# Decay sums of the second block's mixer as 16-row products in two row groups, two head pairs together

## The reference

```
dt = softplus(dt + dt_bias);  a = dt * a_neg                 # per token and head
a_cs = cumsum(a) within a chunk
cb   = einsum('bclgn,bcsgn->bcgls', cc, bc)
m    = cb * exp(where(l >= s, a_cs[l] - a_cs[s], -inf))      # decay between tokens s and l
y    = einsum(m, xs * dt)  (+ what comes over the chunk's border, + d_skip * xs)
y    = rmsnorm(y * silu(z)) ;  out = concat(attn, y) @ w_out
```

## Time and profile before

| what | value |
|---|---|
| median of three runs | 1451.77 us (1451.28 to 1452.57) |
| the profiled execution's own time | 1452.29 us |
| its span | 1450.5 us |
| TensorE busy | 1439.6 us, 99% |
| VectorE busy | 917.8 us, 63% |
| ScalarE busy | 803.5 us, 55% |
| granted TensorE clock, mean | 0.999 |

### The profile page before, as it was taken

One profiled execution on the slowest core, in us unless ns is written; L12 is line 12 of the kernel. 1 busy time (PEld: TensorE's weight loads), 2 busy tenths in 40 slices (PEclk: granted clock), 3 DMA queues, 4 the chain that ended last, 5 costly groups with the idle time before them and its releaser, 6 DMA issues.

```text
span 1450.5 us, 20440 instructions
## 1 busy us (share of the span) xinstructions
PE 1439.6 (99%) x8050; PEld 1228.2 (85%) x8050; DVE 917.8 (63%) x1269; ACT 803.5 (55%) x1301; POOL 78.5 (5%) x86
## 2 busy tenths in 40 slices
PE   9999999999999999999999999999999999999998
PEld 8888888888888888888889988888888998888886
DVE  5697765565557877555555778655555678655554
ACT  6775554444467654544445786544445687554443
POOL 0113100000002230000000000000000000000001
PEclk9999999999999999999999999999999999999999
DMA  8644456656375436565664434576564434465661
GB/s 280 214 155 129 144 166 202 201 189 191 91 236 175 145 118 188 175 204 189 189 189 131 133 116 131 174 215 208 183 193 125 155 118 146 154 206 182 188 189 54
DMA packets 178703, 245.49 MB, mean 169 GB/s; under 512 B 18976, under 2 KB 130224, under 8 KB 178608
## 3 DMA queue, kind: packets, MB, share of 16 engines
q1 hardware_dynamic: 178416, 244.11, 53.7%
q10 hardware_dynamic: 192, 0.08, 0.0%
HBM read 243.10 MB, written 1.05 MB: 168 GB/s over the span
## 4 chain that ended last, share of the span: by engine, by line
PE 93%; DVE 3%; ACT 2%; issue 1%; DVEq 0%; ACTq 0%
PE acc L556 18%; PE acc L559 17%; PE acc L562 17%; PE misc L556 10%; PE misc L559 10%; PE misc L562 10%; PE misc L655 3%; DVE w_lo L1404 2%; PE misc L694 1%; PE misc L912 1%; PE misc L718 1%; ACT w_hi L1001 1%; PE misc L852 1%; PE misc L663 1%; ACT arena L1068 1%
## 5 line engine op out<-in xcount | busy, mean ns | idle before, releaser
L1404 DVE TENSOR_TENSOR w_lo<-w_raw,w_hi 128x1024 fp32r<-128x1024 f32 (+3 forms) x472 | 557.2, 1195 | 295.5 <-ACT w_hi L1001 293.2
L1001 ACT ACTIVATE w_hi<-w_raw 128x1024 fp32r<-128x1024 f32 (+3 forms) x472 | 479.2, 1030 | 276.3 <-PE misc L562 164.1
L556 PE MATMUL acc<-w_hi,h_hi 128*128 128x512 f32 (+3 forms) x832 | 208.7, 373 | 1.0 <-ACT w_hi L1001 1.0
L559 PE MATMUL acc<-w_lo,h_hi 128*128 128x512 f32 (+3 forms) x832 | 201.0, 364 | 0.2 <-DVE w_lo L1404 0.2
L562 PE MATMUL acc<-w_hi,h_lo 128*128 128x512 f32 (+3 forms) x832 | 201.0, 364 | 0.0
L556 PE MATMUL misc<-w_hi,h_hi 128*128 128x512 f32 x640 | 175.6, 396 | 0.0
L559 PE MATMUL misc<-w_lo,h_hi 128*128 128x512 f32 x640 | 171.6, 390 | 0.0
L562 PE MATMUL misc<-w_hi,h_lo 128*128 128x512 f32 x640 | 171.5, 390 | 0.0
L559 PEld LDWEIGHTS acc<-w_lo,h_hi 128*128 128x128 f32 x832 | 147.9, 188 | 22.6 <-DVE w_lo L1404 0.7
L562 PEld LDWEIGHTS acc<-w_hi,h_lo 128*128 128x128 f32 x832 | 148.0, 188 | 21.6
L556 PEld LDWEIGHTS acc<-w_hi,h_hi 128*128 128x128 f32 x832 | 142.5, 189 | 21.7 <-ACT w_hi L1001 1.1
(11 more groups left out here) (221 smaller groups left out, 1217.0 us busy)
## 6 DMA issues: line engine op xcount, KB each, us to landing
w_raw<-in_w_in SPq DMA_DIRECT2D x92, 512.0 KB, 4.1
w_raw<-in_w_gate SPq DMA_DIRECT2D x176, 256.0 KB, 2.9
w_raw<-in_w_up SPq DMA_DIRECT2D x176, 256.0 KB, 3.1
w_raw<-in_w_down SPq DMA_DIRECT2D x88, 512.0 KB, 3.5
w_raw<-in_w_out SPq DMA_DIRECT2D x40, 512.0 KB, 3.9
w_raw<-in_w_in SPq DMA_DIRECT2D x32, 388.0 KB, 3.5
w_raw<-in_w_in SPq DMA_DIRECT2D x16, 336.0 KB, 4.2
w_raw<-in_w_proj_a SPq DMA_DIRECT2D x8, 512.0 KB, 4.1
```

What stands on the lines that cost most here:

```text
L556: pe.matmul(dst, st[0][:, k, t * P:(t + 1) * P], rhs, start=first, stop=False)
L559: pe.matmul(dst, st[0][:, k, t * P:(t + 1) * P], rhs, start=False, stop=False)
L1001: act.activation(w_hi[:, g % RING, 0:w], w_raw[:, g % RING, 0:w], ACT.Copy)\
L1404: dve.tensor_tensor(w_lo[:, g % RING, 0:w], w_raw[:, g % RING, 0:w], w_hi[:, g % RING, 0:w].bitcast(F32), ALU.subtract)\
```

## The change

The running sums are also computed the other way round in cs: four products with 16 columns of `dt_a` as weights and `tri` moving give 16 rows (heads) by 256 tokens, once at rows 0 to 15 and once at rows 64 to 79 of cs's bank. VectorE copies both to a new tile `csT`. A head's row is then spread to all 128 rows by a product of 16 rows: one column of the identity, broadcast to 128 weight columns, with `csT`, 256 columns moving. Two pairs are done in one call, alternating between row groups 0 and 64 and the pairs' two banks; the calls for odd pairs are empty. In `order` cr comes in twos, and z1 stands between y0 and cr2. `reader` makes the bank of cs wait for `csT`. VectorE does `exponents` two by two, and the split counts of both engines are changed to fit.

```diff
--- before.py
+++ after.py
@@ -171,8 +171,8 @@
     order = """
         nT0 nT1 qkv0 nT2 nT3 qkv0 qkv1 qkv1 cvT0 cvT1 qkv2 qkv2 xd0 xd0 qkT0 qkT1 qkT2 qkT3 qkT4 xd0 S0 S1 xd0
         xd1 xd1 PT0 PT1 S2 S3 xT0 xd1 O0 O1 xd1 xd2 PT2 PT3 S4 S5 xd2 O2 O3 xT1 xd2 xT2 xd2 PT4 PT5 xd3 O4 O5
-        xd3 attT0 attT1 xT3 xd3 xd3 z0 xT4 xT5 z0 cs z0 z0 xsT0 xsT2 xsT1 xsT3 cr0 z1 cb0 cb1 cr1
-        z1 y0 cr2 z1 y1 cr3 z1 y2 cr4 wo0 y3 cr5 wo0 y4 cr6 wo1 y5 cr7 ssT0 ssT1 wo1 y6 y7 wo0 wo0 wo1
+        xd3 attT0 attT1 xT3 xd3 xd3 z0 xT4 xT5 z0 cs z0 z0 xsT0 xsT2 xsT1 xsT3 cr0 cr1 z1 cb0 cb1
+        z1 y0 z1 cr2 cr3 y1 z1 y2 wo0 cr4 cr5 y3 wo0 y4 wo1 cr6 cr7 y5 ssT0 ssT1 wo1 y6 y7 wo0 wo0 wo1
         ssT2 ssT3 wo1 wo0 wo0 wo1 mT0 mT1 wo1 mT2 mT3"""
     slots = {n: whole(n) for n in ch}
     plan = [slots[n].pop(0) if n in ch else ("misc", n) for n in order.split()]
@@ -253,6 +253,8 @@
 def reader(block, name):
     if block == 0 and name.startswith("oH"):
         return "dve", name
+    if name == "cs":
+        return "dve", "csT"
     if name in [f"S{g}" for g in range(6)]:
         return "dve", f"Sread{name[1:]}"
     return ("act", f"xs{name[3:]}") if name.startswith("xsT") else ("act" if name.startswith(ACT_READS) else "dve", name)
@@ -328,6 +330,7 @@
         rows = sb("rows", [P, P])
         conv = sb("conv", [P, 60])
         arena = sb("arena", [P, 26112])
+        csT = sb("csT", [P, T])
         acc = [ctx.enter_context(nc.psum_tensor(f"acc{i}", [P, 512], F32)) for i in range(4)]
         misc = [ctx.enter_context(nc.psum_tensor(f"misc{i}", [P, 512], F32)) for i in range(4)]
         ident = const[:, C_ID:C_ID + P]
@@ -843,14 +846,27 @@
                     b = bank_of(layer, name)
                     pe.matmul(b[:, 0:16], tri, dt_a[:, 0:16], start=True, stop=True)
                     pe.matmul(b[:, 16:32], tri, dt_a[:, 16:32], start=True, stop=True)
-                    pe.matmul(b[:, 32:48], bc(tri[:, P - 1:P], [P, P]), dt_a[:, 0:16], start=True, stop=True)\
-                        .then_inc(*PE.mark(name))
+                    pe.matmul(b[:, 32:48], bc(tri[:, P - 1:P], [P, P]), dt_a[:, 0:16], start=True, stop=True)
+                    for t in range(NT):
+                        for r0 in (0, 64):
+                            mm = pe.matmul(b[r0:r0 + SH, 64 + t * P:64 + (t + 1) * P], dt_a[:, 16 * t:16 * t + 16],
+                                           tri, start=True, stop=True)
+                    mm.then_inc(*PE.mark(name))
                 elif kind == "cr":
-                    b = bank_of(layer, name)
-                    for n, (hd, t) in enumerate((hd, t) for hd in (2 * i, 2 * i + 1) for t in range(NT)):
-                        a = dt_a[:, 16 * t + hd:16 * t + hd + 1]
-                        mm = pe.matmul(b[:, n * P:(n + 1) * P], bc(a, [P, P]), tri, start=True, stop=True)
-                    mm.then_inc(*PE.mark(name))
+                    if i % 2:
+                        return
+                    if i == 0:
+                        pe.wait_ge(*DV_.at(layer, "csT"))
+                    banks = [bank_of(layer, f"cr{i + k}") for k in range(2)]
+                    last = []
+                    for u in range(2):
+                        for k in range(2):
+                            r0, hd = 64 * k, 2 * (i + k) + u
+                            last.append(pe.matmul(banks[k][:, u * T:(u + 1) * T],
+                                                  bc(ident[r0:r0 + SH, r0 + hd:r0 + hd + 1], [SH, P]),
+                                                  csT[r0:r0 + SH, :], start=True, stop=True))
+                    last[-2].then_inc(*PE.mark(name))
+                    last[-1].then_inc(*PE.mark(f"cr{i + 1}"))
                 elif kind == "y":
                     pe.wait_ge(*DV_.at(layer, f"M{i}"))
                     if i in (0, 4):
@@ -1282,7 +1298,7 @@
 
                     j = PAIRS.index(hp)
                     if hp:
-                        split_until(layer, ORD[1].before["misc", f"cr{hp}"] + (2 if hp == 1 else LOOK))
+                        split_until(layer, ORD[1].before["misc", f"cr{hp}"] + (0, 3, LOOK - 1, LOOK - 1, LOOK, LOOK, LOOK, LOOK)[hp])
                     b = misc[ORD[1].turn[f"cr{hp}"] % 4]
                     act.wait_ge(*DV_.at(layer, f"cr{hp}"))
                     E = Ex[j % 3]
@@ -1857,7 +1873,9 @@
                 convolve(4)
                 dve.wait_ge(*PE.at(layer, "cs"))
                 b = misc[ORD[1].turn["cs"] % 4]
-                dve.tensor_copy(cs, b[:, 0:48]).then_inc(*DV_.mark("cs"))
+                dve.tensor_copy(cs, b[:, 0:48]).then_inc(*DV_.mark())
+                for r0 in (0, 64):
+                    dve.tensor_copy(csT[r0:r0 + SH, :], b[r0:r0 + SH, 64:64 + T]).then_inc(*DV_.mark("csT"))
                 dve.wait_ge(*AC.at(layer, "log_dt"))
                 dve.wait_ge(*DV_.now(layer))
                 dve.tensor_tensor(dt_v, dt_v, cs[:, 0:32], ALU.subtract).then_inc(*DV_.mark())
@@ -1865,6 +1883,7 @@
                 dve.tensor_tensor(ncx, dt_v[:, 0:16], cs[:, 32:48], ALU.add).then_inc(*DV_.mark())
                 convolve(5)
                 exponents(0)
+                exponents(1)
                 for g in range(2):
                     dve.wait_ge(*PE.at(layer, f"cb{g}"))
                     b = misc[ORD[1].turn[f"cb{g}"] % 4]
@@ -1910,17 +1929,15 @@
                                                  op0=ALU.mult, op1=ALU.mult).then_inc(*DV_.mark(f"ys{g}"))
 
                 for hp in range(SH // 2):
-                    if hp + 1 < SH // 2:
-                        if hp:
-                            split_until(layer, ORD[1].before["misc", f"cr{hp + 1}"] + (2 if hp == 1 else LOOK))
+                    if hp and hp % 2 == 0:
+                        split_until(layer, ORD[1].before["misc", f"cr{hp}"] + (LOOK - 1 if hp == 2 else LOOK))
+                        exponents(hp)
                         exponents(hp + 1)
                     weighted_decays(hp)
                     if hp == 0:
-                        split_until(layer, ORD[1].before["misc", "cr1"] + 2)
+                        split_until(layer, ORD[1].before["misc", "cr1"] + 3)
                     if 1 <= hp < SH // 2 - 1:
                         head_pair_out(hp - 1)
-                    if hp == 1:
-                        split_until(layer, ORD[1].before["misc", "cr2"] + LOOK)
                     if hp == 4:
                         times_silu(0)
                     if hp == 5:
```

## The result

The changed kernel takes 1457.16 us (median of 6 runs, 1455.45 to 1458.48), the kernel before 1451.53: a ratio of 1.0037 with a 95% interval of 1.0025 to 1.0049, +5.6 us. The profiled execution took 1458.04 us for a span of 1456.2. I forecast 1454.8, slower, from three stalls, in a range of 1450.5 to 1457.0: the sign is right, the measured median lies 0.16 us above the range. The rest of the distance is a fourth thing that I had not foreseen.

A forecast was written before the change was run, and what follows sets the result against it. TensorE is 99% busy, but the round through VectorE and ScalarE was to set the pace: per layer -2.2 work, -0.43 old stall, +1.1 +1.2 +1.8 stalls, 0.1 restart give +1.5; two layers +3.0, so 1454.8 us, range 1450.5 to 1457.0.

The forecast's parts named there:

- three stalls: New TensorE waits per layer in the mixer: 1.1 us before y2, 1.2 before y4, 1.8 before ssT1.
- TensorE's own work: Mixer, per layer: four new calls 4.28 us and cs 0.5 added, 6.96 of old sums removed, so -2.2 us.
- Copies hidden: Two VectorE copies into csT after cs, about 0.4 us each, cost nothing; without cover 0.8 us.
- The round sets the pace: In the mixer, sums through VectorE, ScalarE and VectorE to y, not TensorE's work, set the end: +1.5 us per layer.
- The bank at ssT1: ssT1 takes cr6's bank and waits for ScalarE's last read there, ending at 893.74 us: a 1.8 us stall.
- Rival B: Last stall smaller because cr6's bank is read sooner than laid out: +0.5 to +2.0 us, about 1453.2; chance 0.19.
- rival A: The main case: the round sets the pace, +2.0 to +4.0 us, 1453.8 to 1455.8; chance 0.52.
- rival C: Groups don't share for 16-row products or 16-column weights: +3.8 us, 1455.6, with a stall more 1457; chance 0.13.
- the old stall: The kernel before's one gap in TensorE's mixer stretch, 0.43 us ahead of y2, taken to go: -0.43 per layer.
- 0.1 us for the restart: Extra time per layer in the slot behind y7 after the new stalls, taken from the old stall: 0.1 us.
- D: TensorE's work sets the pace in the mixer: -5.2 us in all, 1446.6, with half the stalls 1450; chance 0.13.

The follow-up runs named there:

- e6: As e4 (all calls of sums one slot sooner), but each call made of eight old 128-row products and cs as before; 1450.55 us, ratio 0.9993 to the kernel before.
- e4: The changed kernel with all calls of sums one slot sooner and VectorE's and ScalarE's lists laid out for it; 1446.92 us, ratio 0.9969 to the kernel before.
- e1: The kernel before with only cs's four new products and the two csT copies added, csT read by nobody; 1452.88 us, ratio 1.0008 to the kernel before.
- e2: The changed kernel's order and lists, with cs as before and calls of eight old 128-row products; 1453.38 us, ratio 1.0013 to the kernel before.
- e3: The changed kernel with ssT0's four transposes done four times over, filling the wait at ssT1; 1454.51 us, ratio 1.0020 to the kernel before.
- e5: The changed kernel with sums 6 and 7 ahead of the slot, their minima ahead of the gains; 1453.35 us, ratio 1.0017; a further single execution 1453.57 us.
- left column of the table: Kernels in the changed order, over the kernel before: old products +1.55 us; 16-row products +5.6, or +2.7 with the clock kept.
- right column: Kernels with all calls of sums one slot sooner, over the kernel before: old products -1.06 us, 16-row products -4.7 us.
- e7: The changed kernel with ssT0's transposes done twice, a third of the fill in e3; 1454.14 us, ratio 1.0019 to the kernel before.

## Why the prediction was right, and what it left out

- **TensorE's own work.** Right in its prices. Calls 1.06 us against 1.07 taken, cs 0.55 against 0.5. The saving is real, but smaller than my 2.2 us per layer: e6 less e4 is 1.77 in the length and 3.6 us over both layers, where 4.28 + 0.55 - 6.96 asks for 2.1 and 4.3. About 0.1 us goes ahead of each call (the slot at 865.43 in the changed kernel is followed by the call at 868.38, 2.95 us instead of 2.84), which the layout didn't have.
- **Copies hidden.** Right (e1): 0.85 us of VectorE from 850.12, no wait at xsT3 or cr0.
- **The round sets the pace.** Right, and shown from both sides: with the old products in the same lists a costlier call takes no more time (e2 and e1 together against e3), and with other lists the stalls go and the work counts (e4, e6). The starts of y2, y4 and ssT1 came within 0.1 us of the layout. The idle times in the profile are shorter than my stalls (0.73, 0.76 and 1.42 for 1.1, 1.2 and 1.8), for two reasons. TensorE comes to these steps 0.1 to 0.2 us later than laid out, so that from start to start the stalls are 0.88, 0.92 and 1.63 (the slot at 870.80 plus 2.84 is 873.64, and y2 starts at 874.52). And the idle time begins only at the last record's end, 0.15 to 0.2 us behind that. VectorE idles 1.25 to 1.26 us ahead of the weightings of pairs 2, 4 and 6, where I had 1.35.
- **The bank at ssT1.** Right: the release is L1307, ScalarE's read of cr6's bank, and e5 removes the wait by moving that pair alone. Rival B falls with it.
- **Size.** I forecast +3.0 us, measured +5.6. That is above rival A's own range (1453.8 to 1455.8) and 0.16 us above the whole range, so the mechanism and the sign were right and the size wasn't. The number alone lies nearest to rival C with one stall more (1457), whose mechanism the runs refute. With the clock kept (e3) it is +2.7 and +1.45 per layer in the length, where I had +1.5. In that sum two terms were off against each other: from start to start, TensorE's own work fell by about 1.4 us per layer in this order instead of 2.2 (57.00 less the old stall, against 58.45 less the new ones), and the new stalls came to 3.4 us instead of 4.1, the old one to 0.59 instead of 0.43. That these cancel is no luck: the round sets the starts of y2, y4 and ssT1, and work that isn't saved is time that isn't waited.
- **The step that is missing.** I never asked whether a stall may cost more than its idle time. The term "0.1 us for the restart" stood for it, taken from a stall of 0.43 us; behind the 1.42 us at ssT1 the slot alone was 1.31 us too long in the first layer and 0.91 in the second. Against e3, where the clock stays, the whole lengths are 1.60 us (60.05 and 58.45) and 1.27 us (59.72 and 58.45) longer. Together that is 2.9 us, what lies between +2.7 and +5.6. It is the sum of one execution, though, at 1458.04 us, and the six runs don't all agree with it: three took 1458.0 to 1458.5, two 1456.0 to 1456.3, and one 1455.45 at a mean clock of 0.999, as if two, one and no layer had lost the clock. Only the first of them was profiled, so that is not shown.
- **Rivals C and D.** C is refuted by the 1.06 us and 0.55 us. D is refuted for the changed order, and it is what e4 does in another: the -5.2 us that I wrote for it came out as -4.7. The rule of the Trainium skill, TensorEngine Tiling (Array Packing), PSUM Bottleneck, that tiling doesn't speed up the emptying of PSUM and that this may become the limit, fits the left column of the table. In the right column the same emptying, at the same price (two minima take 1.28 us in the one and 1.29 in the other), is no limit. What decided was its place in the lists.
- **Still open.** What decides whether the clock falls at a given wait. Only e3, e7, the two profiles of e5 and the spread of the runs speak of it. The idle time alone doesn't: e7 keeps waits of 0.74, 0.75 and 0.99 us in its first layer and none of its runs shows a loss, while e5, with 0.75, 0.76 and 0.29, shows one in some.

## What to carry to other kernels

When TensorE is nearly full, write down the round trip of each shared step (sums, minimum, exponentials, weighting, output) on the engines that run strictly down a list, before making its products cheaper. In the changed order the sums of pairs 2, 4 and 6 stood nearer to their first consumer, and the time that the products saved was taken back by the wait; in pairs too, but one slot sooner, they cost no wait. Fix the order and the lists first, then the products. Here the two together gave 4.7 us; the lists with the old products gave 1.06, not set apart from no change, and the new products in the changed order cost 5.6.

A wait of TensorE that can't be removed may be worth filling even with useless products: 0.44 us of transposes per layer brought +5.6 down to +2.5 us. That is shown for this one wait of 1.42 us. The waits of 0.91 (e2) and 0.99 us (e7) had the full clock behind them in their profiles.

## What the hardware showed that I had not expected

- The granted clock fell to 0.50 at 1.42 us of idle time that followed two of 0.73 and 0.76 in the 20 us before, for about 3.4 us (893.9 to 897.3), although TensorE was busy for 28.09 of the 31 us around it. With 0.99 us left of that idle time (e7), and with it filled (e3), it didn't fall, in a profile each.
- The fall doesn't stand at the same place of the wait. In the first layer the clock is still 1.00 during the idle time and falls as ssT1 starts; in the second it falls some 0.7 us into the idle time; in the second execution of e5 it is 1.00 until 887.3, 2.5 us after y4 had ended the wait, with TensorE at work in between.
- It isn't the same in each execution: the six runs of the changed kernel span 3.0 us with mean clocks from 0.997 to 0.999, and one kernel (e5) showed 1.00 and 0.73 behind the same wait of 0.76 us in two executions. The two kernels in which a fall was seen have the wide spreads (3.0 and 2.9 us); e2, e3 and e7 also wait and spread by 1.3 to 1.6 us, about as the kernel before (1.5 us).
- Products of 16 rows in row groups 0 and 64 cost 1.06 us for four of 256 columns, no less than the 1.07 us of those of 64 rows: the rows not used bring nothing.
